# Stick-breaking attention: gates by exponential, one added, reciprocal and product instead of a tangent with two table loads

## What is computed

```python
z = einsum('bqhd,bkhd->bhqk', qb, kb) * scale
log_beta = log_sigmoid(z)
log_1mb = where(causal, log_sigmoid(-z), 0.0)
later = cumsum(log_1mb, axis=3, reverse=True) - log_1mb
w = where(causal, exp(log_beta + later), 0.0)
out = einsum('bhqk,bkhd->bqhd', w, vb)
...
y_sb = y_sb * silu(sb_g)          # silu(g) = g * sigmoid(g)
```

## Time and profile before

| | us |
|---|---|
| runs of the kernel before, median of 3 | 3015.4 (3014.9 to 3016.08) |
| the profiled execution, its own time | 3016.52 |
| its span in the trace | 3014.7 |
| the stick-breaking part in the trace | about 2500 to 2811 |
| PE busy in the span | 2944.7 (98%) |
| DVE busy | 2141.8 (71%) |
| ACT busy | 1243.3 (41%) |

### The profile page before, as it was taken

How to read it: one execution, slowest core, us unless ns; L and a number is a source line. 1 busy time by engine, 2 the same in 40 slices (tenths; PEclk the granted TensorE clock), 3 DMA queues, 4 the chain that set the end, 5 groups by cost and what they waited for, 6 DMA issues and landing times.

```text
span 3014.7 us, 35197 instructions
## 1 busy us (share of the span) xinstructions
PE 2944.7 (98%) x13886; PEld 2311.4 (77%) x13896; DVE 2141.8 (71%) x3303; ACT 1243.3 (41%) x2121; POOL 89.9 (3%) x70
## 2 busy tenths in 40 slices
PE   8999999999999999999999999999999999999998
PEld 7885567878888888888887778888888786566666
DVE  7746866687777777689964977777777725566675
ACT  4215642432222222378842522222223516776652
POOL 0003520000000000000000000000000000000000
PEclk9999999999999999999999999999999999999999
DMA  4330034111111111211141021111111130000213
GB/s 157 112 96 14 1 119 141 34 57 56 49 50 56 49 49 56 102 53 39 53 147 35 27 65 46 53 56 47 52 56 56 63 119 29 22 21 22 98 57 111
DMA packets 72804, 190.47 MB, mean 63 GB/s; under 512 B 8320, under 2 KB 8704, under 8 KB 72512
## 3 DMA queue, kind: packets, MB, share of 16 engines
q1 hardware_dynamic: 72640, 188.23, 19.0%
HBM read 172.20 MB, written 14.68 MB: 62 GB/s over the span
## 4 chain that ended last, share of the span: by engine, by line
PE 84%; DVE 9%; ACT 5%; issue 1%; DMA 0%; POOL 0%; POOLq 0%; DVEq 0%; SPq 0%; ACTq 0%
PE PS L1522 41%; PE PS L279 28%; PE PS L366 2%; PE PS L899 2%; PE PS L320 1%; DVE sm L920 1%; PE PS L885 1%; PE PS L2827 1%; PE PS L2844 1%; PE PS L1110 1%; PE PS L1102 1%; PE PS L911 1%; PE PS L2818 1%; ACT p L938 1%; ACT p L233 1%
## 5 line engine op out<-in xcount | busy, mean ns | idle before, releaser
L1522 PE MATMUL PS<-p 128*128 128x512 f32 x5760 | 1316.1, 391 | 11.8 <-DVE p L1691 11.7
L1522 PEld LDWEIGHTS PS<-p 128*128 128x128 f32 x5760 | 1082.5, 188 | 243.6 <-DVE p L1691 12.5
L279 PE MATMUL PS<-p 128*128 128x512 f32 (+1 forms) x4560 | 1058.5, 391 | 19.8 <-DVE p L477 9.3
L279 PEld LDWEIGHTS PS<-p 128*128 128x128 f32 x4560 | 841.5, 189 | 225.8 <-issue 34.7
L1727 DVE TENSOR_TENSOR p<-p,PS 128x512 f32<-128x512 f32 x480 | 327.5, 683 | 69.8 <-PE PS L1522 56.3
L241 DVE TENSOR_TENSOR p<-p 128x1024 fp32r<-128x1024 f32 x138 | 163.7, 1190 | 134.3 <-ACT p L233 134.0
L1329 DVE TENSOR_TENSOR p<-p 128x512 fp32r<-128x512 f32 x224 | 154.0, 688 | 107.5 <-ACT p L1323 106.5
L1667 ACT ACTIVATE p<-p 128x512 fp32r<-128x512 f32 x128 | 80.2, 628 | 358.5 <-DVE p L1716 336.1
L1323 ACT ACTIVATE p<-p 128x512 fp32r<-128x512 f32 x224 | 139.7, 625 | 173.1 <-PE PS L1522 163.6
L233 ACT ACTIVATE p<-p 128x1024 fp32r<-128x1024 f32 x138 | 141.7, 1030 | 163.0 <-PE PS L279 109.6
L938 ACT ACTIVATE p<-PS,sm 128x256 f32<-128x256 f32 (+2 forms) x256 | 127.7, 508 | 161.8 <-DVE sm L926 83.1
(11 more groups left out here) (237 smaller groups left out, 2834.8 us busy)
## 6 DMA issues: line engine op xcount, KB each, us to landing
p<-in_in_dram SPq DMA_DIRECT2D x72, 512.0 KB, 3.5
p<-in_up_dram SPq DMA_DIRECT2D x128, 256.0 KB, 2.6
p<-in_dn_dram SPq DMA_DIRECT2D x128, 256.0 KB, 2.6
p<-in_out_dram SPq DMA_DIRECT2D x42, 512.0 KB, 3.5
p<-in_ada_dram SPq DMA_DIRECT2D x24, 512.0 KB, 3.5
p<-in_x_dram SPq DMA_DIRECT2D x16, 512.0 KB, 7.8
p<-in_kv_dram SPq DMA_DIRECT2D x16, 512.0 KB, 3.5
spill_dram<-p SPq DMA_DIRECT2D x16, 512.0 KB, 4.2
```

What stands on the lines that cost most here:

```text
L279: ins = e.matmul(ps[:, c:c + m], weights(b, j, wi), x[:, c:c + m], start=first and i == 0, stop=end and i == 2)
L1522: ins = e.matmul(PS[:, bank, :], w[:, wi, :], x[:, xi, :], start=start and i == 0, stop=stop and i == 2, skip_group_check=open_)
```

## The change

The gate is made in another way. ACT takes exp(-g) straight from the bank (L2919 still) and then adds one with an Identity whose bias is a column of ones (L2923); between the two it waits for its own result. `ln_exp` is gone from there. DVE takes the reciprocal of it (L2968), waits for its own result, and multiplies by the bank (L2971). The later product has a factor of 1.0 in place of 0.5.

```diff
@@ act_stick
-                    e.activation(SG[:, pr % 2, HALF[hf]], PS[:, 6 + i % 2, :], ACT.Tanh, scale=0.5).then_inc(*A.did(("th", i)))
-                    ln_exp(e)
+                    e.activation(SG[:, pr % 2, HALF[hf]], PS[:, 6 + i % 2, :], ACT.Exp, scale=-1.0).then_inc(*A.did(("ez", i)))
+                    for w in A.need(("ez", i)):
+                        e.wait_ge(*w)
+                    g = SG[:, pr % 2, HALF[hf]]
+                    e.activation(g, g, ACT.Identity, bias=ones[:, 0:1]).then_inc(*A.did(("th", i)))
@@ dve_stick
-                    e.scalar_tensor_tensor(out=SQ[:, pr, cs], in0=PS[:, 4 + hf, :], scalar=0.5, in1=SG[:, pr % 2, cs], op0=ALU.mult,
+                    e.scalar_tensor_tensor(out=SQ[:, pr, cs], in0=PS[:, 4 + hf, :], scalar=1.0, in1=SG[:, pr % 2, cs], op0=ALU.mult,
@@ dve_stick
-                        e.scalar_tensor_tensor(out=g, in0=g, scalar=1.0, in1=ps, op0=ALU.add, op1=ALU.mult).then_inc(*V.did(("sg", x, hf), ("out", i)))
+                        e.reciprocal(g, g).then_inc(*V.did(("sr", x, hf)))
+                        for w in V.need(("sr", x, hf)):
+                            e.wait_ge(*w)
+                        e.tensor_tensor(g, ps, g, ALU.mult).then_inc(*V.did(("sg", x, hf), ("out", i)))
```

## The result

| | before | after |
|---|---|---|
| median of 20 runs, us | 3014.9 (3012.6 to 3017.9) | 3019.3 (3016.8 to 3023.4) |
| span of the profiled execution, us | 3014.7 | 3019.1 |
| stick-breaking stretch in that trace, us | 309.05 | 311.56 |

The ratio is 1.0013, with a 95% interval of 1.0007 to 1.0019: the change costs 3.9 us, between 2.1 and 5.7. A second comparison gave 1.0010 (1.0001 to 1.0018), 0.3 to 5.4 us.

What follows compares the result with a forecast made beforehand. PE was taken to bound the kernel, waiting only for DVE behind gates, so the softplus's start decides. Gate terms -0.60 + 0.66 + 1.08 + 0.76 = +1.90 us on 3015.4 gave 3017.3; range 3013.0 to 3022.5.

Steps and rivals of the forecast that it cites:

- The steeper line: Length of the gate's reciprocal on DVE from other 4-element reciprocals: 3.82 us, giving 3021.1; slower-reciprocal rival, chance 0.12.
- the rate of an ordinary instruction: Lower bound for the gate's reciprocal, at the rate of the gate's present DVE instruction: 0.69 us.
- the far bound: Upper bound for the gate's reciprocal, if all 253 ns of the 16-element one grew with length: 8.1 us, giving 3055.
- the prediction's estimate of 4.37: Gate's reciprocal at eight passes an element: 4.37 us, +10.1, 3025.5; within the slower-reciprocal rival, chance 0.12.
- C: Third of eight gates, next step 1024 wide: softplus forecast 0.20 us sooner, gained by PE, -0.20 us.
- T: Moment the gate's first table load starts in the kernel before; the softplus was forecast at T + 5.18 behind every gate.
- B and D: Second and fourth gates, next step 256 wide: softplus 1.08 us later, costing PE +1.08 and, after 0.32 slack, +0.76.
- The rival of no net effect: The two gates before 256-wide steps don't pass their delay on: 3015.4 to 3016, chance 0.10.
- The quick reciprocal: Rival: reciprocal of 0.69 to some 2 us, so all 5.49 us of PE's waits go: 3009.9, chance 0.05.
- the cap of 5.49: Sum of PE's waits for DVE behind gates, 5.49 us, taken as the most any quicker gate can win.
- the small chance of a measurable gain: Chance that the whole kernel gets faster by 0.2%, 6.0 us: 0.02, for what was overlooked.

## Why the prediction was right

- **What bounds the kernel.** PE's waits in this stretch, and the softplus's start as the one quantity that decides, were right: all of the difference of the stretch but a few hundredths lies in steps at the eight gates. That PE waits behind gates alone was not quite so: there is a wait of 0.20 us at 2549.92, and those at the end of the stretch, but they are the same in both kernels.
- **The reciprocal's length.** 3.35 us from three short reciprocals on one line, 3.353 measured. The steeper line (3.82), the rate of an ordinary instruction (0.69) and the far bound (8.1) were wrong. There was some luck in it: reciprocals of 4 elements take 178 ns in one part of the trace and 167 in another, and for the 178 spoke only that it lay on one line with the other two. Those of 2 and 16 alone would have given 3.33. The Trainium skill (VectorE: DVE Perf Modes, First, the fixed hardware budget) speaks of a repeat count of 8. Read as eight passes an element, which the page doesn't say, it gave the prediction's estimate of 4.37; the trace doesn't agree with that reading.
- **The term that was mis-sized** is the Identity. I took 0.63 us from an activation whose added one is a plain number, and the new one reads it from a column: 0.72. It lies ahead of the reciprocal at all eight gates, and with the plain number the stretch is 0.7 us shorter. With it the sum is 1.90 + 0.7 = 2.6, against 2.5 measured. The softplus behind C started at T + 5.26, where 5.18 was forecast.
- **B and D.** 1.08 and 0.76 forecast, 1.12 and 0.92 measured; the kernel with tangents there loses 0.5 us in all, not 2.5. The rival of no net effect, which lives on these two gates passing nothing on, falls.
- **The quick reciprocal.** The mechanism was right and its price wrong. I added up idle times of PE to 5.49 us and called that the most to be won; the kernel without a reciprocal won 7.6 in the stretch, because waits between the four matmuls of a group are inside its row's length, not in its brackets, and because groups that wait for nothing overlap (0.63 of the surplus at gate C). "Beyond the cap of 5.49", on which the small chance of a measurable gain rested, doesn't hold. Had the reciprocal been quick, the time would have been some 3007 to 3008 and not 3009.9, an estimate from 3015.4 less 7.6 us and from the one time of that kernel, 3006.8.
- **What was not forecast.** The timed difference is 3.9 us with 2.5 of it found in the stretch. Falls of the granted clock behind the stretch, about 1.5 us each, differ from execution to execution in both kernels, and the prediction had no term for them. The clock on record points to about half a fall more in an execution after the change, at twice its standard error. The queue explains 2.5 of the 3.9 us; that the time came out inside the range all the same is owed to the range, 9.5 us wide for the sake of the reciprocal.

## What to carry to other kernels

Count an added instruction where it stands in its engine's queue, not in its engine's busy time: 3.35 us of reciprocal ahead of the next link of a chain cost 10 us over eight gates, and the same work in two halves in idle places cost 0.7. Where a table of exp and ln is loaded anyway, a sigmoid is exp, ln with one added, exp; it needs neither a table load nor a reciprocal. An upper bound on a gain isn't the sum of the bracketed waits; compare the distance from one group's start to the next with the same distance where nothing was waited for.

## What the runs showed of the hardware

- A reciprocal of n elements a partition in fp32 lies on 153 + 6.25 n ns: 166 ns for 2, 253 for 16, 1746 to 1753 for 256 and 3353 for 512. Of 4 elements there are some of 178 ns, on the line, and some of 167. A product of 512 takes 0.69 us.
- The granted clock fell to half (1.2 of 2.4 GHz) at waits of PE of under 2 us: 1.69 us ahead of the slow group in the second trace of before, 1.85 and 1.67 in the first of after. A wait of 1.83 us in the first trace of before wasn't followed by a fall. Waits of 2.69 and 4.29 us put into the chain at gate C came with one. Behind the stretch each costs about 1.5 us.
- A fall of PE's clock can cost less than the time that its matmuls lose, if PE waits for DVE soon after: of 1.1 and 0.9 us at gate C, 0.9 was taken up by the next wait, that of gate D. With two reciprocals at all eight gates 8.0 us were not taken up.
